# An encoder trunk on one core: memory comes in transposed, and its row norm is applied after the product

## What is computed

```python
def rmsnorm(x, g):
    y = x32 * lax.rsqrt(jnp.mean(x32 * x32, axis=-1, keepdims=True) + EPS)
    return (y * g.astype(jnp.float32)).astype(x.dtype)

def memory_attention(q, mem, mem_norm, w_mem_kv, q_norm, k_norm):
    q = rmsnorm(q.reshape(B, S, MEM_HEADS, MEM_HEAD_DIM), q_norm)
    kv = rmsnorm(mem, mem_norm) @ w_mem_kv
    k = rmsnorm(kv[..., :MEM_WIDTH].reshape(B, N_MEM, MEM_HEADS, MEM_HEAD_DIM), k_norm)
    v = kv[..., MEM_WIDTH:].reshape(B, N_MEM, MEM_HEADS, MEM_HEAD_DIM)
```

## Time and profile before

| | |
|---|---|
| median of 3 runs (lowest to highest) | 1434.51 us (1434.31 to 1434.86) |
| the profiled execution, its own time | 1434.05 us |
| its span from first to last instruction | 1432.3 us |
| TensorE busy | 1393.2 us, 97% of the span |
| mean granted clock of TensorE | 0.999 |

### The profile page before, as it was taken

The page is one execution under the profiler, slowest core; times in us unless marked ns, Lnnn a source line. Parts: engine busy times, 40 slices in busy tenths (PEclk is TensorE's granted clock), DMA queues, the critical chain, the costliest instruction groups (busy, mean ns, idle before and its releaser), DMA issues.

```text
span 1432.3 us, 23084 instructions
## 1 busy us (share of the span) xinstructions
PE 1393.2 (97%) x8120; PEld 1236.3 (86%) x8120; DVE 981.5 (69%) x2072; ACT 760.0 (53%) x1823; POOL 412.8 (29%) x535
## 2 busy tenths in 40 slices
PE   7999999999999999999999999999999999998999
PEld 6889889898888888798888898899888888887997
DVE  6555687887655647888664656888877556578883
ACT  7354466555544436666463535656655345366661
POOL 2231252330202223734212213422311112246450
PEclk9999999999999999999999999999999999999999
DMA  6413221114341222222262132121133413122222
GB/s 224 119 49 88 77 69 46 43 50 146 118 133 55 78 71 82 62 65 90 96 198 82 50 94 79 51 62 47 38 103 126 121 49 96 58 77 60 67 71 103
DMA packets 88674, 121.47 MB, mean 85 GB/s; under 512 B 10353, under 2 KB 58865, under 8 KB 88561
## 3 DMA queue, kind: packets, MB, share of 16 engines
q1 hardware_dynamic: 83088, 112.31, 25.9%
q10 hardware_dynamic: 5472, 7.69, 1.8%
HBM read 115.77 MB, written 4.19 MB: 84 GB/s over the span
## 4 chain that ended last, share of the span: by engine, by line
PE 72%; DVE 12%; ACT 9%; issue 4%; POOL 2%; ACTq 1%; DMA 0%; SPq 0%; DVEq 0%; POOLq 0%
PE bank L1509 22%; PE bank L1511 21%; PE bank L1510 21%; PE bank L1555 5%; ACT prob L578 4%; DVE bank L1270 3%; DVE w_lo_t L881 3%; DVE probT L889 2%; POOL rr L1340 1%; ACT w_hi L553 1%; PE bank L1515 1%; PE bank L1516 1%; ACT q_st L575 1%; DVE nmax L1274 1%; POOL rtmp L1339 1%
## 5 line engine op out<-in xcount | busy, mean ns | idle before, releaser
L881 DVE TENSOR_TENSOR w_lo_t<-w_raw,w_hi 128x256 fp32r<-128x256 f32 (+3 forms) x540 | 302.1, 575 | 288.4 <-ACT w_hi L553 276.0
L553 ACT ACTIVATE w_hi<-w_raw 128x256 fp32r<-128x256 f32 (+3 forms) x544 | 268.5, 509 | 334.3 <-PE bank L1511 310.2
L1509 PE MATMUL bank<-w_hi,actT 128*128 128x256 f32 (+3 forms) x1120 | 361.5, 323 | 5.5 <-DVE probT L889 3.4
L1510 PE MATMUL bank<-w_lo_t,actT 128*128 128x256 f32 (+3 forms) x1120 | 359.1, 321 | 0.0
L1509 PEld LDWEIGHTS bank<-w_hi,actT 128*128 128x128 f32 x1120 | 212.5, 190 | 21.7 <-DVE w_lo_t L881 5.6
L1510 PEld LDWEIGHTS bank<-w_lo_t,actT 128*128 128x128 f32 x1120 | 212.6, 190 | 14.3
L1393 POOL TENSOR_TENSOR prob<-prob,rinv 128x256 f32<-128x256 f32 x192 | 137.9, 748 | 283.7 <-DVE rinv L987 283.7
L1511 PE MATMUL bank<-w_hi,brlo 128*128 128x256 f32 (+1 forms) x608 | 189.0, 311 | 0.0
L578 ACT ACTIVATE prob<-bank,nmax 128x256 f32<-128x256 f32 (+2 forms) x256 | 138.3, 551 | 79.3 <-DVE nmax L1181 39.7
L1511 PE MATMUL bank<-w_hi,actT 128*128 128x512 f32 (+3 forms) x512 | 170.1, 332 | 0.0
L1509 PE MATMUL bank<-actT,w_hi 128*128 128x512 f32 x384 | 152.8, 398 | 3.9 <-DVE probT L889 2.3
(11 more groups left out here) (141 smaller groups left out, 2710.7 us busy)
## 6 DMA issues: line engine op xcount, KB each, us to landing
w_raw<-in_w_mem SPq DMA_DIRECT2D x64, 256.0 KB, 2.6
w_raw<-in_w_out SPq DMA_DIRECT2D x112, 128.0 KB, 2.1
w_raw<-in_w_b SPq DMA_DIRECT2D x112, 128.0 KB, 2.1
w_raw<-in_w_b SPq DMA_DIRECT2D x48, 256.0 KB, 2.7
w_raw<-in_w_out SPq DMA_DIRECT2D x40, 256.0 KB, 2.8
w_raw<-in_w_a SPq DMA_DIRECT2D x32, 256.0 KB, 2.7
w_raw<-in_w_a SPq DMA_DIRECT2D x64, 128.0 KB, 2.0
bias<-in_alibi ACTq DMA_DIRECT2D x28, 192.0 KB, 2.3
```

The source lines that it names most:

```text
L553: act.activation(w_hi[:, n % SPLIT, 0:width], w_raw[:, n % RAW, 0:width], ACT.Copy).then_inc(w_hi_done, 1)
L881: dve.tensor_tensor(w_lo_t[:, n % SPLIT, 0:width], w_raw[:, n % RAW, 0:width], w_hi[:, n % SPLIT, 0:width].bitcast(fp32), ALU.subtract).th ...
L1509: nc.tensor.matmul(out, lhs[0], rhs[0], start=start, stop=False, skip_group_check=skip)
L1510: nc.tensor.matmul(out, lhs[0], rhs[1], start=False, stop=False, skip_group_check=skip)
```

## The change

The host hands the kernel a second copy of memory with features in partitions (`mem_cols`), and `mem_in` is filled from it in 4 transfers of 256 KB. `memory_columns` splits it straight from SBUF, times the gain, into `memT`; the 64 transposes of memory are gone, and with them the scaled rows. `memV` and `memK` are thus products of memory rows without their norm. The norm `rr_m` is applied as the scale with which the values leave PSUM (`mem_values`); the keys have a norm of their own for each head, in which that scale cancels but for EPS, for which GpSimd makes `eps_m`.

The sums of squares come from elsewhere. For the first group GpSimd squares `mem_in` (8 pieces of 128x256), and TensorE multiplies these by a column of ones: 16 plain fp32 matmuls with one column each, in the bank `memN`, between `memV` and `memK` of layer 0. For the second group the memory rows come by 2 DMAs of 512 KB behind the first weights, and ScalarE squares them in layer 0 behind the keys (`memory_squares`). In layer 0 the first 24 transposes of `x` now stand inside `memK`, behind its fifth weight tile, and the last 8 behind `memK`; `x` itself is loaded by 4 issues on ScalarE's queue. The queries wait for each `xT` piece by itself, no longer for all 8.

The diff, cut to its core:

```diff
-        xn = [prob[:, 0:D], prob[:, D:2 * D], mem_in[:, 0, :], mem_in[:, 1, :]]
+        mem_flat = mem_in[:].rearrange("p k n -> p (k n)")
+        xn = [prob[:, 0:D], prob[:, D:2 * D], mem_flat[:, 0:D], mem_flat[:, D:2 * D]]
+        mem_rows = xs_of[:, GROUPS - 1, NM:2 * NM]
+        mem_sq = xs_of[:, GROUPS - 1, 0:NM, :].rearrange("p t d -> p (t d)").rearrange("p (k n) -> p k n", n=NMEM)
...
+                    for j in range(NT):
+                        load_mem_columns(L, j)
+
+                def load_mem_columns(L, j):
+                    sp.dma_start(mem_in[:, 2 * j:2 * j + 2, :], mem_cols[L // 2, :, 2 * j:2 * j + 2, :]).then_inc(mem_loaded[j], 16)
+
+                def load_mem_rows(j):
+                    sp.dma_start(mem_rows[:, j, :], mem[GROUPS - 1, j * P:(j + 1) * P, :]).then_inc(mem_rows_in[j], 16)
+
+                def load_x_rows(G, i):
+                    sp.dma_start(xs_of[:, G, i, :], x[G, i * P:(i + 1) * P, :]).then_inc(x_in[i], 16)
                 def load_x(G):
+
+                    sp.wait_ge(ssm_ready, NM)
+                    sp.wait_ge(*full(("memN", 0)))
                     for i in range(NT):
-                        sp.dma_start(xs_of[:, G, i, :], x[G, i * P:(i + 1) * P, :]).then_inc(x_in[i], 16)
+                        load_x_rows(G, i)
...
+                for j in range(NT):
+                    load_mem_columns(0, j)
+                    if j < 2:
+                        load_weights(2 * j, 2 * j + 2)
                 load_weights(RAW, FIRST["qmem", 0, NT - 1])
                 for dst, src in ((g_in[:, 0, :], rope_gq.partition_broadcast(P)), (g_in[:, 1, :], rope_gk.partition_broadcast(P)),
                                  (sinks[:], sink.partition_broadcast(P)), (cs_in[:, 0, :, :], cos), (cs_in[:, 1, :, :], sin)):
                     sp.dma_start(dst, src).then_inc(tables_in, 16)
+                for j in range(NM):
+                    load_mem_rows(j)
...
+                def memory_squares():
+
+                    for j in range(NM):
+                        act.wait_ge(mem_rows_in[j], 16)
+                        act.activation(mem_rows[:, j, :], mem_rows[:, j, :], ACT.Square,
+                                       accum_out=ss_m[:, NM + j:NM + j + 1]).then_inc(ssm_ready, 1)
+
+                def memory_columns(L):
+
                     if L == 0:
-                        w_hi_to(FIRST["memV", 0, NM - 1] + SPLIT)
+                        w_hi_to(1)
                         act.wait_ge(first_in, 32)
                     else:
                         w_hi_to(FIRST["out", L - 1, 1, NT - 1] + SPLIT)
-                    for j in range(KD // 2):
-                        use = ("memT", L, j)
-                        for s in range(2):
-                            k = 2 * j + s
-                            hi(use, memT[:, 0, k, :], bank(use)[:, s * NMEM:(s + 1) * NMEM],
-                               gcol[:, GAIN_AT[f"mem{L % 2}"] + k:GAIN_AT[f"mem{L % 2}"] + k + 1], first=s == 0)
-
-                for dst, src in ((ident[:], ident_in), (gcol[:], gains)):
+                        act.wait_ge(*full(("aO", L - 1, HA - 1) if L % 2 == 1 else ("bO", L - 1, HB - 1)))
+                    for k in range(KD):
+                        act.wait_ge(mem_loaded[k // 2], 16 * (L + 1))
+                        a = GAIN_AT[f"mem{L % 2}"] + k
+                        act.activation(memT[:, 0, k, :], mem_in[:, k, :], ACT.Copy, scale=gcol[:, a:a + 1]).then_inc(hi_done, 1)
+                        if L == 0:
+                            w_hi_to(min(k + 2, SPLIT))
+
+                for dst, src in ((gcol[:], gains), (ident[:], ident_in)):
                     act.dma_start(dst, src).then_inc(first_in, 16)
...
+                        act.wait_ge(rrm_ready, G + 1)
+                        for j in range(NM):
+                            use = ("memV", L, j)
+                            hi(use, v0[:, 0, 2 * j:2 * j + 2, :], bank(use)[:].rearrange("p (a b) -> p a b", a=2),
+                               rr_m[:, NM * G + j:NM * G + j + 1])
+
                     if L == 0:
-                        memory_rows(0)
-                    w_hi_to(FIRST["memV", L, NM - 1] + SPLIT + 2)
+                        memory_columns(0)
+                        for i in range(NT):
+                            act.dma_start(xs_of[:, 0, i, :], x[0, i * P:(i + 1) * P, :]).then_inc(x_in[i], 16)
+                            w_hi_to(RAW + 1 + i)
+                        w_hi_to(2 * RAW + 1)
+                    else:
+                        w_hi_to(FIRST["memV", L, NM - 1] + SPLIT + 2)
                     for i in range(NT):
+                        if L == 0:
+                            w_hi_to(2 * RAW + 2 + i)
                         act.wait_ge(x_in[i], 16 * (G + 1)) if l == 0 else act.wait_ge(*read(("out", L - 1, 1, i)))
                         row_squares(xs, i)
-                        w_hi_to(FIRST["memV", L, NM - 1] + SPLIT + 3 + i)
-                    for j in range(NM):
-                        use = ("memV", L, j)
-                        hi(use, v0[:, 0, 2 * j:2 * j + 2, :], bank(use)[:].rearrange("p (a b) -> p a b", a=2))
-                    w_hi_to(FIRST["memK", L, NM - 1] + SPLIT)
+                        if L > 0:
+                            w_hi_to(FIRST["memV", L, NM - 1] + SPLIT + 3 + i)
+                    mem_values()
+                    w_hi_to(FIRST["memK", L, NM - 1] + SPLIT + (FIRST_ROWS_AT + 1 if L == 0 else 0))
...
+                def memory_columns(L):
+
+                    w_lo_to(1 if L == 0 else FIRST["out", L - 1, 1, NT - 1] + SPLIT)
+                    for k in range(KD):
+                        a = GAIN_AT[f"mem{L % 2}"] + k
+                        dve.wait_ge(hi_done, count("hi"))
+                        dve.scalar_tensor_tensor(out=memT[:, 1, k, :], in0=mem_in[:, k, :], scalar=gcol[:, a:a + 1],
+                                                 in1=memT[:, 0, k, :].bitcast(fp32), op0=ALU.mult,
+                                                 op1=ALU.subtract).then_inc(mem_split, 1)
+                        if L == 0:
+                            w_lo_to(min(k + 2, SPLIT))
...
                     if L == 0:
-                        memory_rows(0)
-                    w_lo_to(FIRST["memV", L, NM - 1] + SPLIT + 2)
-                    dve.wait_ge(xn_ready, count.n["rrx"])
+                        memory_columns(0)
+                        w_lo_to(2 * RAW + 1)
+                    else:
+                        w_lo_to(FIRST["memV", L, NM - 1] + SPLIT + 2)
                     for i in range(NT):
+                        if L == 0:
+                            w_lo_to(2 * RAW + 2 + i)
+                            if i == FIRST_SUMS_AT:
+                                dve.wait_ge(*full(("memN", L)))
+                                dve.tensor_copy(ss_m[:, 0:NM], bank(("memN", L))[:, 0:NM]).then_inc(read(("memN", L))[0], 1)
                         row_norm(xs, i)
-                        w_lo_to(FIRST["memV", L, NM - 1] + SPLIT + 3 + i)
...
+                    if G == 0:
+                        pool.wait_ge(*read(("memN", 0)))
+                    else:
+                        pool.wait_ge(ssm_ready, NM)
+                    link(nc.gpsimd.tensor_scalar(eps_m[:, at], ss_m[:, at], EPS / D, EPS * EPS, ALU.mult, ALU.add))
+                    rsqrt(ss_m[:, at], rr_m[:, at], NM, D, rrm_ready)
...
+                    if L == 0:
+                        for k in range(KD):
+                            pool.wait_ge(mem_loaded[k // 2], 16)
+                            pool.tensor_tensor(mem_sq[:, k, :], mem_in[:, k, :], mem_in[:, k, :], ALU.mult).then_inc(mem_sq_done, 1)
+                    else:
+                        w_lo(FIRST["memV", L, NM - 1] + 3)
                     for i in range(NT):
+                        if L == 0 and i == FIRST_SUMS_AT:
+                            memory_scales(0)
                         rows([i])
-                        if MEM_LO[4 + i] == "pool":
-                            w_lo(FIRST["memV", L, NM - 1] + 4 + i)
-                    batches(MH, MD, NM)
+                    batches(MH, MD, NM, eps_m[:, G * NM:(G + 1) * NM])
...
+
+                    def mem_chunk(part, after={}):
                         def operands(k, j, w):
-                            pe.wait_ge(*read(("memT", L, k // 2)))
+                            if j == 0:
+                                pe.wait_ge(mem_split, mem_split_count(L, k))
                             return (memT[:, 0, k, j * P:(j + 1) * P], memT[:, 1, k, j * P:(j + 1) * P]), w
-                        project([(part, L, j) for j in range(NM)], KD, operands, lambda use: bank(use)[:])
-
...
+                        project([(part, L, j) for j in range(NM)], KD, operands, lambda use: bank(use)[:], after)
+
...
+                    mem_chunk("memV")
+                    if L == 0:
+                        pe.wait_ge(ones_set, 1)
+                        pe.wait_ge(*vacant(("memN", L)))
```

(19 more changed lines are left out.)

150 lines of the change are left out of this document (73 added, 77 removed).

## The result

The change takes 1437.13 us at the median (1434.81 to 1439.73, 12 runs) where the kernel before takes 1434.49 us beside it (1433.56 to 1435.22, 12 runs): a ratio of 1.0020, 95% interval 1.0011 to 1.0029. It is slower by 0.2%, 2.6 us, where 1428.4 us was forecast, 6.1 us less than the kernel before.

A forecast was written before the change was run, and what follows sets the result against it. TensorE was taken as the bound, busy for 1393.2 of 1432.3 us. From the profiled 1434.05, 5.25 us (boundaries) and 0.9 (start) came off, giving 1427.9, or 1428.4 us at the median; range 1425.0 to 1431.7.

The forecast's parts named there:

- 5.25 us for the boundaries: Three sets of 16 memory transposes in the middle, 1.75 us each on TensorE's chain, vanish with nothing replacing them there.
- 0.9 us for the start: Layer 0's start up to the queries: they begin at 39.8 where it was 40.68.
- The step that failed most: Start: the extra 1 MB on SyncE's queue ahead of the query weights, and ScalarE's later squares, cost nothing.
- the rival *slower: First 30 us: late weight landings starve values and keys, losing 8.7 us plus 1.6 of slow clock; 1438.7 us; chance 0.03.
- The tightest place: First query blocks, needing the bank of the seventh xT piece once copied: 0.4 us of wait, between 0 and 1.0.
- The three waits in the keys' chain: Keys of layer 0: third row block of x ready 4.9 us after the sums, TensorE there after 6.9, 2.0 left.
- First product and values: Start: first product at 7.3 (6.9 to 8.5); values take 11.0 us plus 2.0 of slow clock, ending at 20.3.
- Sums: Between values and keys: 16 plain fp32 one-column matmuls at 0.273 us each take 4.4 us, bounds 1.75 and 7.0.
- The single stretch at the start: From the first product on: one slow-clock stretch of some 4 us at half speed, 2.0 us lost, bounds 1.5 and 3.1.
- the rival *eaten start: TensorE counts as idle in the sums, so keys start at half speed, 1.7 us lost; 1431.6 us in all; chance 0.10.
- 1.4 us of cover. I take nothing: Boundaries: four memory issues instead of two cost nothing ahead of the output weights; slower small transfers would cost only their excess.
- the likeliest case: Whole kernel: the forecast of 1428.4 us, between 1426.8 and 1430.0, with chance 0.56.

The follow-up runs named there:

- kernel 1: The change with the second group's 1 MB of memory rows and their squares behind the query and gate weights: 1433.39 us, 0.9992 of the kernel before.
- kernel 5: The change with the first two copies of xT ahead of the first query weight's split on ScalarE and VectorE: 1434.97 us, 1.0003 of the kernel before.
- kernel 6: The edit of kernel 5 together with the later memory rows of kernel 1, on the change: 1432.17 us, 0.9987 of the kernel before.
- kernel 4: The change with memory rows later, memory's columns in contiguous blocks and the sums spread over the values: 1432.82 us, 0.9985 of the kernel before.
- kernel 7: Kernel 4 plus the copies order of kernel 5 and the keys' fifth tile's low part ahead of the third row scaling: 1432.55 us, 0.9984.
- kernel 11: The change with one of GpSimd's eight squarings of memory, read eight times by the sums: 1437.44 us, 1.0021 of the kernel before.
- kernel 2: The change with memory's columns laid out so each of 4 transfers reads one contiguous 256 KB: 1434.63 us, 1.0004 of the kernel before.
- kernel 3: The change with two of the 16 sums behind each weight tile of the values, not all in a row: 1436.86 us, 1.0015 of the kernel before.
- kernel 8: The change with layer 0 taken back to memory by rows and transposes, and the second group's rows late: 1430.15 us, 0.9968 of the kernel before.
- kernel 9: Kernel 8 with the second group's x loaded behind the output weights, directly ahead of layer 1's query weights: 1430.11 us, 0.9969 of the kernel before.
- kernel 12: Kernel 8 with the second group's x loaded behind layer 1's weights up to its key and value projection: 1429.23 us, 0.9965 of the kernel before.
- kernel 10: Kernel 9 with memory's columns in contiguous blocks of 256 KB: 1430.00 us, 0.9967 of the kernel before.

## Why the prediction was wrong

Its sum had two terms, 5.25 us for the boundaries and 0.9 us for the start. Measured are 3.10 and -5.20.

**The step that failed most** reads "The extra 1 MB of memory rows passes SyncE's queue ahead of the query weights, and ScalarE squares it later ...: nothing." I had costed the squaring, which is indeed hidden, and not the transfer. The first query weight was issued at 31.18, was wanted by ScalarE at 33.4 and came at 39.27. By the medians the transfer's price is 3.7 us (the change against kernel 1) and 2.8 (kernel 5 against 6), where the whole loss is 2.6; the edit moves the squares of these rows along with them. The intervals of these ratios reach some 0.1% either way, 1.3 us, so that the step failed is shown and its exact size isn't. Nor is the whole wait the megabyte's: without it, in kernel 1, ScalarE still waited 5.3 us for the weight, behind the five tables. I had worked out such a landing rule myself, in the rival *slower* ("It decides from a landing of ... 4.2 us on"), but put it at the values and keys, where it cost little (0.64 us at 20.36), and not at the tile behind the megabyte, where a single landing of 8.1 us was enough.

**The tightest place** was named rightly, the copies of the last pieces of `xT`, with 0.4 us "between 0 and 1.0". It took 0.56 + 0.33 + 0.32 ahead of the queries and 2.17 inside them, 3.4 us: the copies stand on ScalarE behind the split of that weight, which the count of instructions didn't show. Kernels 5 and 6 show both halves, the order and the landing: either edit alone leaves 2.17 or 2.16 us, both together 0.39.

**The three waits in the keys' chain.** The 2.0 us of slack for the third row block held in the change itself, since the keys were slowed by the clock. Where the clock stayed up in the keys, the slack is below zero: TensorE waited 1.26 us there in kernel 1, 1.29 in 5 and 1.67 in 6. The chain took longer than the 4.9 us that I put behind the sums (which end at 25.35), and in the profiled executions of kernels 4, 6 and 7, which stay at 1432 to 1433 us, the wait for it is the longest that is left (2.12, 1.67 and 2.33 us). VectorE's rows in the change:

```profile
26.54 0.15 DVE L1102 COPY ss_m<-bank 128x2 f32<-128x2 f32 x1
29.05 0.75 DVE L996 TENSOR_SCALAR mem_in<-xs,rr_x 128x1024 f32<-128x1024 f32 x1 [2.35 <-POOL rr_x L1415]
```

The third row is scaled 3.7 us behind the sums and the fourth, at 31.12, 5.8. The fourth row's squares come late as well: ScalarE begins them at 28.67, behind a weight split that waited 2.33 us for TensorE.

**First product and values.** 7.78 for 7.3 and 14.1 for 13.0, inside the bounds. Of the excess of 1.1 us in the values the late weight at 20.36 is the larger part, since kernels 1, 5 and 6, without that wait, took 13.1 to 13.4. GpSimd's squares, which I had counted as free because nobody waits for GpSimd, do take time from VectorE, but kernel 11 shows no more than 0.6 us of it on TensorE and none on the first product. "SBUF — State Buffer" of the Trainium skill, section "SBUF: two separate sides", states that a VectorE operation with two SBUF inputs and a GpSimd operation that reads SBUF exclude each other for a whole instruction. Both low parts here, of a weight and of a piece of memory, are of that kind, and kernel 11 agrees in that they stretch (0.68 to 1.10 us).

**Sums.** 3.5 us for 4.4, within the bounds, 0.9 won. The row counts 32 matmuls where the program has 16: a plain fp32 product is carried out as two, 0.11 us each, the pace of a transpose. The Trainium skill's figure from "TensorE: Matmul & The Clock Gate", section Terms, four times that pace, would have made 7.0 us; the measurement decides for twice, for a product of one column. It says nothing of that factor between a transpose and a product of as many columns.

**Slow clock.** The single stretch at the start is there (0.63 us a product from 8.35 to 11.33), and the rival *eaten start* came true as well: a second stretch in the first keys, nine products in 3.7 us instead of 2.2, so 1.5 us. Its reason (that TensorE counts as idle in the sums) isn't shown and isn't refuted. Of the six profiled executions with the sums in one row, three (the change, 2 and 11) had a stretch right behind them, kernel 11 without a wait before it, and three (1, 5 and 6) had none there. Kernel 3 had two further on without the row of sums. Kernels 4, 5 and 7 had one behind a wait of 2.1 to 2.3 us, at 31, 47 and 35 us, and kernel 2 a second at 48, behind one of 2.18; but the change, 1 and 11 had a wait of 2.2 us in the queries and no stretch behind it. Kernels 8, 9 and 12 had none, and 10 only one in the values, as the kernel before.

This is a cause of the same order as the late weight, and the record has a figure for it. The mean granted clock of the change's twelve executions is 0.996 to 0.999, 0.9983 on average. It is 1.000 in all 26 of kernels 8, 9, 10 and 12 and in 80 of 86 of the kernel before beside the experiments. An estimate from that: (1 - 0.9983) x 1434 = 2.4 us lost at the low clock in an execution, up to 0.7 either way since the figures are rounded. The six executions of the change at 0.999 average 1436.3 us, the six below it 1438.4. In kernel 1 the average is 0.9988, so some 0.7 of its 3.7 us may be clock. How far the late weight and the waits bring the slow stretches on was not tested. The spread of single executions (4.9 us in the change) is no sign of them: the kernel before spread over 3.8 us in 31 executions and 4.7 in 18, nearly all at 1.000.

**Boundaries.** The 1.75 us on the chain were right as a price: 1.44, 1.81 and 1.55 in kernel 12. The cover that I took for memory's transfers ("1.4 us of cover. I take nothing") was too small at the first boundary alone, where 2 MB of `x` stand between memory and the output weights: 1.3 us lost in kernel 8 against 12. The `x` stood there before too, so the risk that the forecast named, slower small transfers, is the likely reason and not a shown one; laid out in blocks, in kernel 2, they leave ScalarE 6.03 us of that wait. In the change this shows in ScalarE's row:

```profile
363.24 0.63 ACT L596 ACTIVATE w_hi<-w_raw 128x512 fp32r<-128x512 f32 x1 [6.31 <-DMA w_raw<-in_w_out]
```

6.9 us later than in the earlier trace rows, when everything else is 5.1 later. What is missing at the others in the change, 0.4 and 0.3 us, stays open. There is a new wait of the last transposes of `x` on the copies of the values, which now carry a scale and come at the end (0.23 us at 401.02 in the change), but kernel 12 has it too and wins 1.81 and 1.55 there. It was not tested by itself.

So the likeliest case missed through a transfer that was priced at nothing, an order that put eight copies behind it, and a second slow stretch. The rival *slower* came true only in its sign: its gaps in the values and keys are not what happened. The chance of 0.03 for slower was far too small for a start in which so many orders were changed at once. What was never reached is a start by columns that equals the old one: the best of these, kernel 6, begins the gates at 64.01, 1.6 us later than before (62.44).

## What to carry to other kernels

When a transfer is put into a queue that feeds weights, price it at the next tile of that queue and not by the engine that uses it: issue time, what stands ahead, landing, and then every instruction that stands behind that tile in its engine's program. Data that is wanted layers later belongs where weights are used slowly; here moving 1 MB to such a place was worth 3.7 and 2.8 us in two pairs of kernels, and moving 2 MB 1.3 us at the boundary behind it, of which the medians show 0.9, within their noise. When several orders change at once, keep the one that removes work (here 1429.2 to 1430.2 us for the boundaries alone) and test the start apart from it.

## What the hardware showed

- A plain fp32 matmul of 128x128 by one column is recorded as two matmuls, 0.22 us together; 16 took 3.5 us.
- Beside GpSimd's fp32 squares from SBUF, VectorE's operations with two SBUF inputs took 1.10 us in place of 0.68, and 0.83 in place of 0.47.
- While five transfers of small tables (8 to 128 KB) were under way, the whole core moved 4 to 28 GB/s for 4.4 us, with 1 MB and a weight queued behind them. The kernel before has a like stretch; there ScalarE waited 0.73 us for the weight behind it, and TensorE not at all.
- At the start products can be 0.63 us long with a granted clock of 1.00 in the window: the column doesn't show every slow stretch. Kernel 10 has the same from 12.46 to 16.43. This is the change:

```profile
7.80:11.50 3.70, 3.70 (x9) 2.93 (x10) 3.70 (x5) 3.63 (x9) 3.55 (x5) 1.00 0.94 302
```
